# Filler products on TensorE ahead of four of its waits, in a one-core step of a hybrid decoder

## The reference

```python
# layer 0: one input projection, split between two mixers
q, k, v = latent attention (8 heads, rotary tail, RMSNorm of every head)
sample attention also reads 8 cached pages of 128 positions for each sequence
gated linear attention (4 heads of 128, chunks of 64, exact recurrence)
h = h + concat(heads) @ w_out
# layer 1: S5, a diagonal complex state-space layer
y = Re(C scan(B u)) + D u ; h = h + GLU(GELU(y))
# behind each mixer
h = h + square(relu(rmsnorm(h) @ w_up)) @ w_down          # 4096 wide
h = h + sigmoid(rmsnorm(h) @ w_gate) * (p[i] @ w_proj)    # per-layer embedding
```

## Time and profile before

| | us |
|---|---|
| median of 3 runs | 989.92 (987.89 to 990.01) |
| profiled execution | 985.38 |
| its span, first to last instruction | 983.7 |
| PE busy | 943.7 (96%) |
| DVE busy | 632.6 (64%) |
| ACT busy | 473.8 (48%) |
| POOL busy | 128.7 (13%) |
| mean granted clock of PE | 0.982 |

### The profile page before, as it was taken

One profiled execution on the slowest core, in us unless ns is written; L12 is line 12 of the kernel. 1 busy time (PEld: TensorE's weight loads), 2 busy tenths in 40 slices (PEclk: granted clock), 3 DMA queues, 4 the chain that ended last, 5 costly groups with the idle time before them and its releaser, 6 DMA issues.

```text
span 983.7 us, 17735 instructions
## 1 busy us (share of the span) xinstructions
PE 943.7 (96%) x6831; PEld 868.4 (88%) x6831; DVE 632.6 (64%) x1118; ACT 473.8 (48%) x834; POOL 128.7 (13%) x220
## 2 busy tenths in 40 slices
PE   6999999989999799999999989899999999999997
PEld 6998478779888489999999977688999999999997
DVE  5653897788687268975585554399766666443453
ACT  6433465664335145755342546236666655433353
POOL 3420141000014220000000318900000000000000
PEclk9999999999879999999999999999999999999999
DMA  8580032211327754444444420500444444434431
GB/s 327 191 317 18 26 92 87 87 54 53 110 82 220 259 191 142 162 169 172 171 166 152 158 83 1 215 12 1 154 171 171 155 155 166 167 153 154 156 140 49
DMA packets 34485, 135.42 MB, mean 138 GB/s; under 512 B 5273, under 2 KB 17433, under 8 KB 21858
## 3 DMA queue, kind: packets, MB, share of 16 engines
q1 hardware_dynamic: 28370, 117.37, 33.1%
q0 software_dynamic: 6032, 16.92, 5.4%
HBM read 130.11 MB, written 4.17 MB: 136 GB/s over the span
## 4 chain that ended last, share of the span: by engine, by line
PE 73%; DVE 11%; POOL 5%; issue 5%; ACT 2%; DMA 2%; POOLq 1%; SPq 0%; DVEq 0%; ACTq 0%
PE ps L891 18%; PE ps L893 18%; PE ps L892 18%; POOL arena L794 4%; PE ps L923 3%; PE ps L1096 2%; PE ps L1097 1%; PE ps L1098 1%; DMA ring<-in_stream 1%; PE ps L1019 1%; POOLq L713 1%; DVE const L2576 1%; DVE sq L2582 1%; PE ps L1212 1%; DMA arena<-in_ckv 1%
## 5 line engine op out<-in xcount | busy, mean ns | idle before, releaser
L893 PE MATMUL ps<-a2hi_split,ring_split 128*128 128x288 f32 x512 | 150.5, 294 | 0.0
L893 PEld LDWEIGHTS ps<-a2hi_split,ring_split 128*128 128x128 f32 x512 | 96.4, 188 | 0.0
L891 PE MATMUL ps<-nhi_split,hi_split 128*128 128x288 f32 x320 | 95.2, 297 | 0.1
L893 PE MATMUL ps<-nhi_split,ring_split 128*128 128x288 f32 x320 | 94.1, 294 | 0.0
L1976 DVE TENSOR_TENSOR ring_split<-ring,hi_split 128x2048 fp32r<-128x2048 f32 x36 | 82.2, 2285 | 17.3 <-ACT hi_split L1547 17.3
L1547 ACT ACTIVATE hi_split<-ring 128x2048 fp32r<-128x2048 f32 x36 | 68.7, 1911 | 31.1 <-PE ps L893 22.7
L1096 PE MATMUL ps<-sq_split,hT_split 128*128 128x288 f32 (+1 forms) x256 | 80.1, 313 | 3.5 <-DVE pages_lo_split L2143 3.3
L1097 PE MATMUL ps<-wuk_lo_split,hT_split 128*128 128x288 f32 (+1 forms) x256 | 76.6, 299 | 0.0
L1098 PE MATMUL ps<-sq_split,pages_lo_split 128*128 128x288 f32 (+1 forms) x256 | 76.6, 299 | 0.0
L891 PE MATMUL ps<-up_nhi_split,up_hi_split 128*128 128x288 f32 x256 | 76.2, 298 | 0.1
L891 PE MATMUL ps<-a2hi_split,hi_split 128*128 128x288 f32 x256 | 75.8, 296 | 0.0
(11 more groups left out here) (427 smaller groups left out, 2601.0 us busy)
## 6 DMA issues: line engine op xcount, KB each, us to landing
ring<-in_stream SPq DMA_DIRECT2D x96, 1024.0 KB, 4.8
arena<-in_ckvT SPq DMA_DIRECT2D x64, 128.0 KB, 2.1
arena<-in_ckv POOLq DMA_DIRECT2D x26, 128.0 KB, 3.1
ring<-in_ckv POOLq DMA_DIRECT2D x21, 128.0 KB, 2.4
arena<-in_wu POOLq DMA_DIRECT2D x1, 2240.0 KB, 11.0
arena<-in_ckv SPq DMA_DIRECT2D x17, 128.0 KB, 3.1
arena<-in_s POOLq DMA_DIRECT2D x4, 512.0 KB, 3.7
out_gla_s<-arena POOLq DMA_DIRECT2D x4, 512.0 KB, 2.9
```

The source lines that it names most:

```text
L891: pe.matmul(ps[:, 0:T], wh[:, k, col:col + P], xh, start=first and k == which[0], stop=False)
L893: mm = pe.matmul(ps[:, 0:T], wl[:, k, col:col + P], xh, start=False, stop=last and k == which[-1])
```

## The change

`keep_busy` moves to the top of PE's program and takes the moving operand as an argument. It is called at four more places, each ahead of a wait of PE: five products ahead of pair 15's wait for its split pages, seven ahead of the second `weighted_values`, four ahead of projection 2 of the first embedding, and five ahead of `shifted(0)`. Each writes the bank of the group that comes next there, or of one that comes soon, and overwrites it. No other instruction is added, removed or moved.

```diff
+            def keep_busy(ps, times, x):
+                for _ in range(times):
+                    pe.matmul(ps, ident, x, start=True, stop=True, skip_group_check=True)
...
                     if p == 0:
                         pe.wait_ge(wuk_split, 2)
+                    if p == 15:
+                        keep_busy(bank(("ka", p, j))[:, 0:T], 5, cst("causal")[:, 0:T])
                     if p < AHEAD:
                         pe.wait_ge(first_split, p + 1)
...
             def weighted_values(c):

+                if c == 1:
+                    keep_busy(bank("ol1")[:, 0:T], 7, cst("causal")[:, 0:T])
                 pe.wait_ge(p_all, 2 * c + 2)
...
                 for i in range(8):
+                    if i == 2:
+                        keep_busy(bank(("G", 0))[:, 0:T], 4, p3[:, 0])
                     project(("proj", L, i), wp, P * i, P, D, lambda k: p3[:, k], blocks=2)
...
             sumsq_part(3, 6)
-
-
-            def keep_busy(ps, times):
-                for _ in range(times):
-                    pe.matmul(ps, ident, h3[:, 0], start=True, stop=True, skip_group_check=True)
+            keep_busy(bank(("BT", 12))[:, 0:T], 5, h3[:, 0])

             for i in range(3):
                 shifted(i)
             b_turned(12)
-            keep_busy(bank(("BT", 13))[:, 0:T], 3)
+            keep_busy(bank(("BT", 13))[:, 0:T], 3, h3[:, 0])
             b_turned(13)
...
-            keep_busy(bank(("v5", 0))[:, 0:T], 1)
+            keep_busy(bank(("v5", 0))[:, 0:T], 1, h3[:, 0])
```

More of the change, by code:

```diff
@@ L1445, in outputs @@
                 if i >= 5:
-                    keep_busy(bank(("y5", i + 1) if i < 7 else ("glu_a", 0))[:, 0:T], 3)
+                    keep_busy(bank(("y5", i + 1) if i < 7 else ("glu_a", 0))[:, 0:T], 3, h3[:, 0])
                 pe.wait_ge(samples_in, i + 1)
```

## The result

| | us |
|---|---|
| the change, median of 4 runs | 1014.62 (1011.17 to 1021.08) |
| the change once more, median of 6 runs | 1012.53 (1008.95 to 1017.68) |
| ratio to the kernel before | 1.0264 (95%: 1.0196 to 1.0332) |
| profiled execution (span) | 1021.08 (1019.4), mean granted clock 0.946 |

The account below looks back on a forecast made before the run. PE was busy 96% of the span, but until POOL's release of VectorE not the bound. Terms 0 - 1.7 + 0 + 0 + 1.6 = -0.1 us gave a median of 989.8 us; forecast's own range 988 to 992, full range 986.2 to 1016.

Parts of the forecast that it names:

- the wait that grows: Ahead of the first S5 products: wait grows from 0.95 to 3.4 us, clock falls there, costing about 1.6 us.
- rival 2: At the first S5 products the clock falls and stays down: +26 us, 1014 us; chance 0.27.
- rival 1: Ahead of the first S5 products, the grown wait does no harm: 988.2 us; chance 0.28.
- Site 1: Fillers ahead of pair 15: it runs at full clock, but pair 16 still waits for its split; term 0.
- rival 3: Pair 15's fillers run at half clock, so pair 16 starts 3.9 us late: 992.1 us; chance 0.06.
- Site 2: Second weighted values: fillers keep full clock, second half of L1259 takes 3.69 instead of 5.37 us; term -1.7 us.
- Sites 3 and 4: First embedding's third projection and first shifted residual: faster products, but POOL's release unchanged, PE only earlier; terms 0.
- Rivals 1 and 4: Rival 1 has its own line; the other: fillers do not hold the clock at all, 989.9 us; chance 0.05.

Follow-up runs that it names:

- e3: The change with only its fillers ahead of the first shifted residual kept; median 1001.24 us, 3 of 6 runs above 1000.
- e7: Kernel before with three fillers instead of one ahead of the first S5 products and one in each of the first five outputs; median 990.28 us, 4 of 13 above 1016.
- e12: The change with only its fillers in the first embedding and ahead of the first shifted residual; six of six runs above 1007 us.
- e10: As e9, with six fillers instead of ten in the gated linear attention; ten of 13 runs at 979 to 985 us, three above 1004.
- e1: The change with nine fillers instead of one ahead of the first S5 products; median 988.47 us (981.92 to 1003.98).
- e2: The change with only its fillers ahead of pair 15 and the second weighted values; median 1002.94 us, 3 of 6 runs above 1000.
- e6: As e1, plus one filler in each of the first five outputs of S5; median 988.88 us (980.89 to 997.90), none of 12 above 1000.
- e5: The change itself run once more, unaltered; median of 6 runs 1012.53 us, all above 1008.
- e9: The change without pair 15's fillers, with nine ahead of S5, one in each of its first five outputs, ten in the gated linear attention; median 981.63 us.
- e4: The change with only its seven fillers ahead of the second weighted values; median 1014.40 us, 4 of 6 runs above 1000.
- e11: The kernel before itself, run again unaltered; 6 of 12 runs above 1010 us, profiled run 987.33.

## Why the prediction was wrong

**The step that failed** is the price of the wait that grows: "a stretch of 3.3 us like the one in rows 3 loses 3.3 x (1 - 1/1.88) = 1.55 us". It took the length of a fall from a place with dense products of 288 columns right behind it. The fall of rows 3 was over at 634.40, and six records of fillers stand in it (timeline of PE, the kernel before):

```profile
633.20 2.25 PE L1413 MATMUL ps<-hT,const 128*128 128x288 f32 x6
```

Behind the first S5 products there is nothing like that up to `outputs(5)`; the only products of 288 columns are those of `shifted`, eight short records with 32 output rows at a time. The clock stayed at 0.50 for 64.75 us, and the term measured 26.9 us, not 1.55. That is rival 2, with its place, its mechanism and its price (+26), to which I gave 0.27. Its range held the time, and the forecast did not. That rival 2's time (1014 us) came within 1 us of the median (1014.62) is in part luck: its sum has nothing for the gated linear attention, and counts from the lower level of the kernel before. To the upper one (median 1013.92) the change is no slower.

The argument that misled was "the same stage stays at 1.00 today, so it does not pull the clock down by itself". Staying at full clock and coming back to it are different things: e3, e7 and e12 show the same products at 0.50 until the fillers of `outputs(5)`. And it stays at full clock behind the waits of 0.91 and 0.71 us that it has in its middle today; in e10 and e1 waits of 1.66 and 1.75 us there were each followed by 0.50.

**The baseline.** I read one execution and three runs as the kernel's time. Its runs have two levels, and on the upper one it does already what the change does always. The page that I cited in rival 1 (the Trainium skill, TensorE: Matmul & The Clock Gate, Part 1: the monitor is not started with the kernel, so cold products differ from run to run) bears on this. The runs agree in that the same wait brings a fall in one and none in another (2.65 us in the earlier trace rows, 2.64 us in e7); what the monitor saw no run shows. I used it to mix forecast and rival 1, and did not ask whether the kernel before was mixed as well.

**Site 1**: term 0 expected, fillers at full clock. They began at 216.63, as worked out, after 2.0 us of idle time, and then ran at half clock, as in rival 3 (so in e2 and e6 too; in e1 and e5 the same ten records took 2.69 us). The timeline of PE:

```profile
216.63 4.38 PE L884 MATMUL ps<-const 128*128 128x288 f32 x10 [2.01 <-DVE arena L2162]
220.63 0.51 PE L1100 MATMUL ps<-sq_split,hT_split 128*128 128x288 f32 x1
...
223.87 0.30 PE L1100 MATMUL ps<-sq_split,hT_split 128*128 128x288 f32 x1
```

Pair 15 starts 2.6 us later than in the earlier trace rows, but at full clock, so pair 16 (223.87 against 223.06) is 0.8 us late and not rival 3's 3.9. e9 does without site 1.

**Site 2**: right in size. 64 records in 3.70 us (e4; 3.70 in the change), 1.7 us less than in the earlier trace rows. The clock fell there in four of the five traces without these fillers, not in e12, and in none of the nine with them. That the 1.7 us are kept to the end is not shown: the two low runs of e4 (987.52 and 990.18) do not lie below those of the kernel before (ratio 1.0005, 0.994 to 1.007).

**Sites 3 and 4**: right in that they win nothing. From POOL's L782 to the release of VectorE it was 51.0 us (587.11 to 638.09) and is 51.3 us (595.58 to 646.86), with PE early or late. PE came about 3.5 us earlier relative to that release, not 2.5, so the wait became 4.40, above my 2.3 to 4. Wrong was to call that "PE is only earlier": being late was what protected the S5 stage.

**Rivals 1 and 4** did not come: in no trace did S5 keep its clock behind a wait of over 2 us, and the fillers of sites 2 to 4 did hold it.

The second loss, 254 to 295 us, was not in the prediction, and is not shown to belong to the change: every trace without fillers there has 10 to 41 us at 0.50 in that stage, those with site 1 (e1, e2, e5, e6: 30.7, 10.2, 30.7, 30.7) and those without it (e3, e4, e7, e11, e12: 30.7, 27.3, 20.5, 20.5, 13.7).

## What to carry to other kernels

Before a wait is filled or shortened, look where the time goes next: PE that comes earlier to an event set by another engine only waits there instead, and the wait has moved to a place with thinner products behind it. Price a fall of the clock by the products behind it, up to the next dense ones, and put fillers at the wait that stays, as many as fit the length to which it grows; fillers at the waits in front of it alone made things worse (e12), and with those in front open, three at the wait that stays did not fit it when PE came early (e7). And read the spread of the runs before the median: the two levels of the kernel before have a cause that could be found and removed. With the falls in the gated linear attention that took the median from 1011.79 to 981.63, in one set of runs.

## What was not expected of the hardware

The same wait at the same place (2.64 and 2.65 us) was followed by half clock in one execution and by full clock in another. The S5 products, most of them 71 and 72 columns wide, ran for 34 us at 1.00 when they began there and for up to 70 us (e7) at 0.50 when they began there, with PE busy for about 95% of the time or more in both. The clock came back each time during the six records of fillers in `outputs(5)` or within 1.4 us behind them; the two records in each output of e7 and e10 did not bring it back. In that stage a wait of 1.66 us was followed by a fall, while 2.64 us ahead of products of 288 columns was not (e7). In both traces where the clock fell in the middle of the stage (e1, e10), a read of 256 KB from DRAM that landed 1.5 to 1.9 us later than in the others stood at the head of it.
